# Feed-forward tokens in blocks of 512, 512 and 32 columns instead of three of 352, in a hybrid decoder step

## The reference

```python
def finish_layer(x, o_n, o_f, g_n, g_f, w_o, g_post_mix, g_pre_ffn, g_post_ffn, w_gate, w_up, w_down):
    mixed = jnp.concatenate([rms_norm(o_n, g_n), rms_norm(o_f, g_f)], axis=-1) @ w_o
    x = x + rms_norm(mixed, g_post_mix)
    hf = rms_norm(x, g_pre_ffn)
    ffn = (jax.nn.silu(hf @ w_gate) * (hf @ w_up)) @ w_down
    return x + rms_norm(ffn, g_post_ffn)
```

## Time and profile before

| | |
|---|---|
| median of 3 runs | 2107.08 us (2105.73 to 2108.0) |
| profiled execution, its own time | 2104.82 us |
| its span, first to last instruction | 2103.1 us |
| mean granted TensorE clock | 0.928 |
| TensorE busy | 1812.2 us, 13367 matmuls |
| VectorE busy | 955.6 us |
| ScalarE busy | 586.9 us |
| gate and up stage | 1257.1 to 1763.5 us, 3168 matmuls |
| down stage | 1771.4 to 2043.5 us, 1584 matmuls |

### The profile page before, as it was taken

One profiled execution on the slowest core, in us unless ns is written; L12 is line 12 of the kernel. 1 busy time (PEld: TensorE's weight loads), 2 busy tenths in 40 slices (PEclk: granted clock), 3 DMA queues, 4 the chain that ended last, 5 costly groups with the idle time before them and its releaser, 6 DMA issues. The chain is left out here.

```text
span 2103.1 us, 35222 instructions
## 1 busy us (share of the span) xinstructions
PE 1812.2 (86%) x13367; PEld 1615.7 (77%) x13367; DVE 955.6 (45%) x1830; ACT 586.9 (28%) x1173; POOL 210.2 (10%) x454
## 2 busy tenths in 40 slices
PE   7799998898849998999659319999999998999983
PEld 6799997765626676767459319999999998999982
DVE  4423332234526777667673571212222123655558
ACT  4100002212306565656522120100110011333341
POOL 3000041405312111111100000000000000000000
PEclk8999999999959999999779759999999999999996
DMA  6436855559990122100031031111111110111113
GB/s 220 147 93 154 218 126 131 187 172 292 326 235 10 43 50 55 38 1 2 21 112 30 10 108 44 44 46 49 41 50 40 50 40 26 42 45 42 45 56 134
DMA packets 163054, 188.02 MB, mean 89 GB/s; under 512 B 30887, under 2 KB 129562, under 8 KB 162226
## 3 DMA queue, kind: packets, MB, share of 16 engines
q1 hardware_dynamic: 136914, 140.74, 21.8%
q0 software_dynamic: 13152, 37.24, 6.7%
q10 hardware_dynamic: 12864, 8.39, 1.8%
HBM read 151.78 MB, written 38.71 MB: 91 GB/s over the span
## 5 line engine op out<-in xcount | busy, mean ns | idle before, releaser
L176 PE MATMUL psum<-hf_hi,gu_hi 128*128 128x352 f32 x1056 | 341.8, 324 | 35.5 <-DVE gu_lo L2517 35.5
L177 PE MATMUL psum<-hf_lo,gu_hi 128*128 128x352 f32 x1056 | 339.5, 322 | 0.0
L178 PE MATMUL psum<-hf_hi,gu_lo 128*128 128x352 f32 x1056 | 339.1, 321 | 0.0
L176 PEld LDWEIGHTS psum<-hf_hi,gu_hi 128*128 128x128 f32 x1056 | 199.0, 188 | 36.5 <-issue 36.5
L177 PEld LDWEIGHTS psum<-hf_lo,gu_hi 128*128 128x128 f32 x1056 | 199.2, 189 | 0.0
L178 PEld LDWEIGHTS psum<-hf_hi,gu_lo 128*128 128x128 f32 x1056 | 198.7, 188 | 0.0
L176 PE MATMUL psum<-h_hi,down_hi 128*128 128x352 f32 x528 | 174.1, 330 | 19.4 <-DVE h_lo L2616 19.4
L176 PE MATMUL psum<-x_hi,w_hi 128*128 128x352 f32 x528 | 172.0, 326 | 8.9 <-DVE w_lo L635 4.5
L177 PE MATMUL psum<-h_lo,down_hi 128*128 128x352 f32 x528 | 172.6, 327 | 0.0
L178 PE MATMUL psum<-h_hi,down_lo 128*128 128x352 f32 x528 | 172.3, 326 | 0.0
L177 PE MATMUL psum<-x_lo,w_hi 128*128 128x352 f32 x528 | 171.6, 325 | 0.0
(11 more groups left out here) (361 smaller groups left out, 3260.7 us busy)
## 6 DMA issues: line engine op xcount, KB each, us to landing
fox_ring<-in_cache_fox_kv SPq DMA_DIRECT2D x128, 256.0 KB, 6.1
zT<-z_stage SPq DMA_DIRECT2D x22, 528.0 KB, 2.9
w_ring<-in_w_in POOLq DMA_DIRECT2D x22, 512.0 KB, 5.4
gu_ring<-in_w_ffn_gate SPq DMA_DIRECT2D x22, 512.0 KB, 3.9
gu_ring<-in_w_ffn_up SPq DMA_DIRECT2D x22, 512.0 KB, 3.8
down_ring<-in_w_ffn_down SPq DMA_DIRECT2D x44, 256.0 KB, 2.6
nsa_page<-in_cache_nsa_kv POOLq DMA_DIRECT2D x64, 128.0 KB, 6.3
out<-nat SPq DMA_DIRECT2D x12, 512.0 KB
```

The source lines that it names most:

```text
L176: nc.tensor.matmul(dst, w_hi, x_hi, start=start, stop=False)
L177: nc.tensor.matmul(dst, w_hi, x_lo, start=False, stop=False)
L178: return nc.tensor.matmul(dst, w_lo, x_hi, start=False, stop=stop)
```

## The change

A table of three slices takes the place of the even thirds: tokens 0 to 511, 512 to 1023 and 1024 to 1055. A helper `width` gives a block's columns. All instructions of `build_e` that go by blocks follow: the matmuls of both stages, silu, the product with silu, and the copies at the end of an output group. Blocks, their banks, the order of loops, buffers and waits stay. Other stages keep blocks of 352.

```diff
@@ -2449,6 +2449,14 @@
                         nc.vector.tensor_copy(y_nat[0:n, t, b * 512:(b + 1) * 512], psum[0:n, 4 + j % 4, :]).then_inc(copied, 1)
 
 
+BLOCKS = (slice(0, 512), slice(512, T), slice(T, N))
+
+
+def width(b):
+
+    return BLOCKS[b].stop - BLOCKS[b].start
+
+
 def build_e(nc, a, env, hf_hi, hf_lo, yT):
 
 
@@ -2488,8 +2496,8 @@
                             pe.wait_ge((silu_ready, h_ready)[s], f + 1)
                             for b in range(3):
                                 for k in range(KD):
-                                    tok = slice(b * NB, (b + 1) * NB)
-                                    last = product(nc, psum[:, 3 * s + b, 0:NB], w_hi[:, s, k, :], w_lo[:, s, k, :],
+                                    tok = BLOCKS[b]
+                                    last = product(nc, psum[:, 3 * s + b, 0:width(b)], w_hi[:, s, k, :], w_lo[:, s, k, :],
                                                    hf_hi[:, k, tok], hf_lo[:, k, tok], k == 0, k == KD - 1)
                             last.then_inc(done[s], 1)
 
@@ -2500,7 +2508,7 @@
                         act.wait_ge(done[0], f + 2)
                         act.wait_ge(h_ready, f + 1)
                         for b in range(3):
-                            last = nc.scalar.activation(silu[:, b * NB:(b + 1) * NB], psum[:, b, 0:NB], ACT.Silu)
+                            last = nc.scalar.activation(silu[:, BLOCKS[b]], psum[:, b, 0:width(b)], ACT.Silu)
                         last.then_inc(silu_ready, 1)
 
                 @block.vector
@@ -2521,7 +2529,7 @@
                         dve.wait_ge(silu_ready, f + 2)
                         for b in range(3):
                             dst = hT[:, f, :] if isinstance(f, int) else hT[:, bass.ds(f, 1), :].rearrange("p o n -> p (o n)")
-                            last = nc.vector.tensor_tensor(dst[:, b * NB:(b + 1) * NB], psum[:, 3 + b, 0:NB], silu[:, b * NB:(b + 1) * NB], ALU.mult)
+                            last = nc.vector.tensor_tensor(dst[:, BLOCKS[b]], psum[:, 3 + b, 0:width(b)], silu[:, BLOCKS[b]], ALU.mult)
                         last.then_inc(h_ready, 1)
 
                     split_tile(0, 0)
@@ -2578,9 +2586,9 @@
                                 pe.wait_ge(h_split, g * FG + (q + 1))
                                 for c in range(2):
                                     for b in range(3):
-                                        tok = slice(b * NB, (b + 1) * NB)
+                                        tok = BLOCKS[b]
                                         col = slice(c * P, (c + 1) * P)
-                                        last = product(nc, psum[:, 3 * c + b, 0:NB], w_hi[:, s, q, col], w_lo[:, s, q, col],
+                                        last = product(nc, psum[:, 3 * c + b, 0:width(b)], w_hi[:, s, q, col], w_lo[:, s, q, col],
                                                        h_hi[:, q, tok], h_lo[:, q, tok], f == 0, f == FT - 1)
                                 last.then_inc(used, 1)
 
@@ -2595,8 +2603,8 @@
                             if step == STEPS - 1:
                                 act.wait_ge(used, g * FG + 3 * FG)
                                 for b in range(3):
-                                    last = nc.scalar.copy(yT[:, bass.ds(i * 4 + half * 2, 1), b * NB:(b + 1) * NB].rearrange("p o n -> p (o n)"),
-                                                          psum[:, b, 0:NB])
+                                    last = nc.scalar.copy(yT[:, bass.ds(i * 4 + half * 2, 1), BLOCKS[b]].rearrange("p o n -> p (o n)"),
+                                                          psum[:, b, 0:width(b)])
                                 last.then_inc(y_copied[0], 1)
 
                 @block.vector
@@ -2617,8 +2625,8 @@
                             if step == STEPS - 1:
                                 dve.wait_ge(used, g * FG + 3 * FG)
                                 for b in range(3):
-                                    last = nc.vector.tensor_copy(yT[:, bass.ds(i * 4 + half * 2 + 1, 1), b * NB:(b + 1) * NB].rearrange("p o n -> p (o n)"),
-                                                                 psum[:, 3 + b, 0:NB])
+                                    last = nc.vector.tensor_copy(yT[:, bass.ds(i * 4 + half * 2 + 1, 1), BLOCKS[b]].rearrange("p o n -> p (o n)"),
+                                                                 psum[:, 3 + b, 0:width(b)])
                                 last.then_inc(y_copied[1], 1)
                     dve.wait_ge(y_copied[1], 5)
 
```

## The result

The changed kernel takes 2268.13 us (median of 4 runs, 2265.88 to 2268.71), the one before 2107.54 us (2105.73 to 2109.0) beside it. The ratio is 1.076, 95% interval 1.0742 to 1.0779: 160.6 us slower, where +146 had been forecast. The profiled execution has a span of 2265.9 us, 162.8 over the one before.

A forecast was written before the change was run, and what follows sets the result against it. TensorE's matmuls were taken to bound both feed-forward stages. Matmul sets +143 us and clock falls 3 us make +146 on the profiled 2104.8, so 2250.8; with the median 2.3 us higher, 2252 us was predicted, range 2225 to 2325.

The forecast's parts named there:

- What bounds the kernel: Gate and up stage and down stage: each lasts as long as its TensorE matmuls, plus four fixed gaps in the latter.
- the sum is on the path: Both feed-forward stages: all the added matmul time, +143 us, lengthens the kernel, as no other engine was awaited there.
- Step 2: 32-column matmuls in both feed-forward stages: each takes 110 ns, its weight load sticking out; bounds 14, 54 and 189 ns.
- Step 1: 512-column matmuls in both feed-forward stages: 228.5 ns each, between 225.5 (surplus by instruction) and 231.1 (by column).
- The sum: Both feed-forward stages: a set of three matmuls goes from 476.7 to 567.0 ns, times 1584 is +143 us.
- Step 4: ScalarE and VectorE at tile ends: silu, its product and copies out of PSUM cost nothing; 1 us if that were off.
- Step 5: TensorE's clock behind 44 short stretches of mostly weight loads in the gate and up stage: 2 falls, 3 us.
- the rival: Gate and up stage: the clock falls behind each of 44 short stretches, 70 us more, 2322 us; chance 0.07.
- No overlap: Narrow matmuls in both feed-forward stages: load and matmul don't overlap, 189 ns each, +268 us, 2375 us; chance 0.07.
- short loads: Narrow matmuls in both feed-forward stages: loads as quick as half-width ones, 54 ns, +54 us, 2161 us; chance 0.06.
- faster: Each set of three: surplus paid by instruction, narrow matmul's load hidden, 13.3 ns; -20 us, 2087 us; chance 0.03.
- no difference: Each set of three: time goes by columns alone, 0.451 ns each, loads hidden; 476.7 ns, 2107 us; chance 0.03.

## Why the prediction was right, and where it was off

- *What bounds the kernel* and *the sum is on the path*: right. TensorE's waits are the same five, and the stages grew by 107 and 51 us where 95 and 48 were forecast.
- *Step 2, the narrow matmul has the length of a load*: right, 111.4 ns for the 110 taken, +2 us. Halving the load halved the step, and 96 columns cost what 32 do.
- *Step 1, the wide matmul*: off by 3.5 ns. I took 228.5, between "by instruction" (225.5) and "by column" (231.1); it is 232.0, a little over the upper end and over the 225 to 231 that were to show it. Two of them in 1584 sets are 11 us, most of the miss. The stream of the earlier trace rows, which spoke for the columns, should have weighed more. The bf16 run shows where the surplus sits.
- *The sum*: a set takes 575.2 ns, +98.5 on 476.7, times 1584 is +156; with three or four falls of the clock (5 to 6 us) +161 to +162, against 160.6 measured. The forecast of 2252 is a little under its own terms: 2250.8 and 2.3 make 2253.
- *Step 4, copies and silu cost nothing*: right. TensorE's waits at the group ends are 19.6 us for 20.6.
- *Step 5, the clock*: two falls put down, three and four seen. The argument against the rival was wrong, though: that TensorE never pauses did not keep the clock up. It fell behind three and four of the 44 short stretches; why behind these is not shown.
- *Rivals.* No overlap (2375), short loads (2161), faster (2087) and no difference (2107) are out by the steps above. The faster rival's condition, a short matmul under 25.7 ns, holds for bf16 (25), but there most of the surplus is gone that two large matmuls were to save on. The set of 456.6 ns that was worked out beside this rival is what bf16 parts gave (456), not what this kernel has.

## What to carry to other kernels

In these stages a matmul lasts as long as the longer of two things: its own columns, and the load of the next one's weights. With fp32r that load is 111 to 112 ns for 128 columns, so a block under about 250 columns (112/0.45, an estimate; runs had 32, 96 and 256) pays for columns that it does not have. Cut N into even blocks rather than full ones and a remainder: 400, 400 and 256 cost 0.6% of the kernel's time, 480, 480 and 96 cost 5.1%, and 512, 512 and 32, a remainder of 3% of the columns, 7.6%. What it costs depends on the type of the operands: with bf16 the last of these cuts cost 0.8%.

## What was not expected

- The clock fell behind 3.4 us in which TensorE was busy throughout, with 27 matmuls, 22 of them narrow, and 3.23 us of loads. With 96 columns in place of 32 and runs of the same length it stayed at 1.00 through the stage, in one profile.
- bf16 loads of 128 columns follow one another after 25 ns, less than a quarter of the fp32r distance; twice the speed was expected.
- fp32r matmuls of 352 and 512 columns run at 0.451 to 0.453 ns per column, bf16 ones at 0.42. At 352 columns that alone was worth 52 us of 2108.
- 256 columns take 119 ns, 0.466 a column, though the load's 112 are over by then; why the surplus is larger there stays open.
- The order of the loops moves a set at full clock too: 571.8 ns with k outside, 575.2 with blocks outside, for the same matmuls. Why stays open.
